# Expert weight loads: the first matrix's loads issued slot by slot from SyncE, the second matrix's from ScalarE's own queue

## What is computed

```python
def expert_block(args):
    xb, e = args
    gu = xb @ w_gu[e] + b_gu[e]                     # w_gu[e]: 1024 x 2048, float32
    g = jnp.minimum(gu[:, :D_EXPERT], SWIGLU_LIMIT)
    lin = jnp.clip(gu[:, D_EXPERT:], -SWIGLU_LIMIT, SWIGLU_LIMIT)
    act = g * jax.nn.sigmoid(SWIGLU_ALPHA * g) * (lin + 1.0)
    return act @ w_down[e] + b_down[e]              # w_down[e]: 1024 x 1024, float32
```

## Time and profile before

| | us |
|---|---|
| median of 3 runs | 1465.5 (1463.52 to 1466.69) |
| the profiled execution, its own time | 1465.08 |
| its span in the trace | 1463.2 |
| TensorE busy | 1431.0 (98% of the span) |
| VectorE, ScalarE, GpSimd busy | 499.0, 323.9, 276.9 |
| q1 (SyncE's loads) | 448.83 MB, 74.4% of 16 DMA engines' span |
| granted TensorE clock, mean | 0.997 |

### The profile page before, as it was taken

The page is one execution under the profiler, slowest core; times in us unless marked ns, Lnnn a source line. Parts: engine busy times, 40 slices in busy tenths (PEclk is TensorE's granted clock), DMA queues, the critical chain, the costliest instruction groups (busy, mean ns, idle before and its releaser), DMA issues.

```text
span 1463.2 us, 34048 instructions
## 1 busy us (share of the span) xinstructions
PE 1431.0 (98%) x14854; PEld 752.4 (51%) x14854; DVE 499.0 (34%) x715; ACT 323.9 (22%) x556; POOL 276.9 (19%) x360
## 2 busy tenths in 40 slices
PE   8999999999989999999999999999999999999997
PEld 7876588888863444444444444444444443333334
DVE  4848833324572223222222222232222222222233
ACT  6458842223121111111111111111111111111111
POOL 0000000000012222233222233222332222332211
PEclk9999999999999999999999999999999999999999
DMA  7330003323969599999999999999999999999987
GB/s 260 146 94 1 23 12 123 96 73 134 362 237 418 215 415 418 414 417 412 413 420 414 416 416 411 417 414 418 418 412 414 417 418 418 418 414 413 416 338 254
DMA packets 77595, 466.72 MB, mean 319 GB/s; under 512 B 23160, under 2 KB 31764, under 8 KB 52944
## 3 DMA queue, kind: packets, MB, share of 16 engines
q1 hardware_dynamic: 50528, 448.83, 74.4%
q0 software_dynamic: 18464, 16.94, 5.3%
q10 hardware_dynamic: 8560, 0.34, 0.3%
HBM read 456.69 MB, written 19.27 MB: 325 GB/s over the span
## 4 chain that ended last, share of the span: by engine, by line
PE 81%; DMA 14%; DVE 3%; issue 1%; ACT 1%; SPq 0%; POOL 0%; ACTq 0%; DVEq 0%; POOLq 0%
PE ps L1783 35%; PE ps L1799 19%; DMA dn_pair<-in_w_down 11%; PE ps L1433 7%; PE ps L1435 7%; PE ps L1434 7%; PE ps L1460 2%; DMA gu_pair<-in_w_gate_up 2%; PE ps L1586 1%; DVE head_max L1092 1%; PE ps L1542 1%; DVE probs L1110 1%; DMA xf<-x_rows 1%; DMA x_rows<-y_sb,sum_row 0%; PE ps L1689 0%
## 5 line engine op out<-in xcount | busy, mean ns | idle before, releaser
L1783 PE MATMUL ps<-gu_pair,xt 128*32 128x512 f32 x6144 | 668.4, 594 | 4.1 <-ACT ps L861 3.0
L1783 PEld LDWEIGHTS ps<-gu_pair,xt 128*32 128x32 f32 x6144 | 204.2, 110 | 448.0 <-issue 427.6
L1799 PE MATMUL ps<-dn_pair,act_t 128*32 128x256 f32 x6144 | 339.2, 379 | 2.5 <-DMA dn_pair<-in_w_down 2.0
L1799 PEld LDWEIGHTS ps<-dn_pair,act_t 128*32 128x32 f32 x6144 | 203.3, 110 | 146.6 <-issue 13.5
L1332 DVE TENSOR_SCALAR lin_sb<-ps 128x768 f32<-128x768 f32 x32 | 30.6, 958 | 584.7 <-ACT sg_sb L852 584.7
L852 ACT ACTIVATE sg_sb<-ps,limits 128x768 f32<-128x768 f32 x32 | 28.8, 901 | 593.5 <-PE ps L1783 593.5
L954 POOL DMA_INDIRECT x_rows<-y_sb,sum_row x93 | 147.0, 1581 | 37.7 <-issue 37.7
L931 POOL TENSOR_TENSOR mark_sb<-ones 1x1 f32<-1x1 f32 x93 | 30.0, 323 | 613.8 <-DVE y_sb L1348 608.7
L1433 PE MATMUL ps<-w_high,h_hi 128*128 128x512 f32 x352 | 138.2, 392 | 0.6 <-DVE mem_lo L1038 0.5
L1435 PE MATMUL ps<-w_high,h_lo 128*128 128x512 f32 x352 | 137.2, 390 | 0.0
L1434 PE MATMUL ps<-w_low,h_hi 128*128 128x512 f32 x352 | 137.0, 389 | 0.0
(11 more groups left out here) (249 smaller groups left out, 1002.6 us busy)
## 6 DMA issues: line engine op xcount, KB each, us to landing
gu_pair<-in_w_gate_up SPq DMA_DIRECT2D x128, 2048.0 KB, 29.0
dn_pair<-in_w_down SPq DMA_DIRECT2D x64, 2048.0 KB, 19.9
w_raw<-in_w_in SPq DMA_DIRECT2D x8, 2048.0 KB, 7.9
w_raw<-in_w_out SPq DMA_DIRECT2D x2, 2048.0 KB, 8.0
w_raw<-in_w_in SPq DMA_DIRECT2D x2, 1024.0 KB, 8.1
x_sb<-in_x SPq DMA_DIRECT2D x8, 256.0 KB, 7.8
w_raw<-in_w_mem_kv SPq DMA_DIRECT2D x1, 2048.0 KB, 12.6
x<-in_x SPq DMA_DIRECT2D x4, 512.0 KB, 5.3
```

What stands on the lines that cost most here:

```text
L1783: last = nc.tensor.matmul(ps[quarter(q), g, :], xt[:, g, k, :], w.rearrange("p (h n) -> p h n", h=2)[:, :, q * QCOLS:(q + 1) * QCOLS], sta ...
L1799: last = nc.tensor.matmul(ps[quarter(q), bank + g, 0:QCOLS], act_part(2 * c + h, g), dn_w[c][:, h * D + q * QCOLS:h * D + (q + 1) * QCOLS] ...
```

## The change

The second-matrix loads are taken out of SyncE's program and put into ScalarE's: `next_dn` in the loop, after `seed(j + 2)`, with the same waits for `down(j)`'s parts, and once more after the loop for job 31. They go through ScalarE's own hardware queue (q10). SyncE keeps the first-matrix loads; their waits from the second turn on are 4 parts lower, and the first turn of the loop is written out ahead of it.

```diff
--- before.py
+++ after.py
@@ -628,23 +628,25 @@
             sp.wait_ge(gate_t_ps, 1)
             load_gu(e_one, 1, GU_PAIRS - 1)
             pairs_but_one = sp.value_load(job_table[0:1, 1, 1:2], min_val=MIN_PAIRS - 1, max_val=NJ // 2 - 1)
-            with sp.Fori(0, pairs_but_one) as i:
+
+            def next_gu(i, b, e_gu):
+                for m in range(GU_PAIRS):
+                    wait_part(sp, i, b * PARTS - DN_PARTS + 2 * m + 1)
+                    load_gu(e_gu, b, m)
+
+            e_two = sp.value_load(job_table[0:1, 0, 2:3], min_val=0, max_val=N_EXP - 1)
+            for m in range(GU_PAIRS):
+                wait_part(sp, 0, 2 * m + 1)
+                load_gu(e_two, 0, m)
+            e_three = sp.value_load(job_table[0:1, 0, 3:4], min_val=0, max_val=N_EXP - 1)
+            next_gu(0, 1, e_three)
+            with sp.Fori(1, pairs_but_one) as i:
                 for b in range(2):
                     e_gu = sp.value_load(job_table[0:1, 0, bass.ds(i * 2 + b + 2, 1)], min_val=0, max_val=N_EXP - 1)
-                    e_dn = sp.value_load(job_table[0:1, 0, bass.ds(i * 2 + b + 1, 1)], min_val=0, max_val=N_EXP - 1)
-                    for m in range(GU_PAIRS):
-                        wait_part(sp, i, b * PARTS + 2 * m + 1)
-                        load_gu(e_gu, b, m)
-                    for m in range(DN_PAIRS):
-                        wait_part(sp, i, stream(b, KD + 2 * m + 1))
-                        load_dn(e_dn, m)
-            e_last = sp.value_load(job_table[0:1, 0, bass.ds(pairs_but_one * 2 + 1, 1)], min_val=0, max_val=N_EXP - 1)
+                    next_gu(i, b, e_gu)
             wait_part(sp, pairs_but_one, stream(0, KD - 1))
             for t in range(TB):
                 sp.dma_start(down_bias[N_EXP * t:N_EXP * (t + 1), :], b_down[0]).then_inc(down_bias_in, 16)
-            for m in range(DN_PAIRS):
-                wait_part(sp, pairs_but_one, stream(0, KD + 2 * m + 1))
-                load_dn(e_last, m)
             sp.wait_ge(act_ready, pairs_but_one * 2 + 2)
             sp.dma_start(final_gain[:], norm_final.rearrange("(a n) -> a n", a=1).to_broadcast([P, D])).then_inc(fgain_in, 16)
             sp.wait_ge(added, pairs_but_one * (32 * TRIOS) + (16 + 16 * TRIOS))
@@ -860,6 +862,9 @@
                     act.wait_ge(gs_ready, j)
                 nc.scalar.activation(ps[:, 0:TRIOS, :], bias_sb[:].rearrange("p (a h) n -> p a (h n)", a=1).to_broadcast([P, TRIOS, COLS]),
                                      ACT.Copy).then_inc(seeded, 1)
+
+            def next_dn(e, m):
+                act.dma_start(dn_pair[m][:], wdn[e, m, :, :]).then_inc(dn_in[m], 16)
 
             def keep_gate(j, b):
                 nc.scalar.activation(y_gate[:, b:b + 1, :], slot_gates[:, bass.ds(j, 1), :], ACT.Copy).then_inc(gate_kept, 1)
@@ -892,10 +897,18 @@
                     wait_part(act, i, stream(b, KD - 1))
                     sigmoid(j + 1)
                     seed(j + 2)
+                    e_dn = act.value_load(job_table[0:1, 0, bass.ds(j + 1, 1)], min_val=0, max_val=N_EXP - 1)
+                    for m in range(DN_PAIRS):
+                        wait_part(act, i, stream(b, KD + 2 * m + 1))
+                        next_dn(e_dn, m)
             keep_gate(pairs_but_one * 2, 0)
             act.wait_ge(act_ready, pairs_but_one * 2 + 1)
             wait_part(act, pairs_but_one, stream(0, KD - 1))
             sigmoid(pairs_but_one * 2 + 1)
+            e_last = act.value_load(job_table[0:1, 0, bass.ds(pairs_but_one * 2 + 1, 1)], min_val=0, max_val=N_EXP - 1)
+            for m in range(DN_PAIRS):
+                wait_part(act, pairs_but_one, stream(0, KD + 2 * m + 1))
+                next_dn(e_last, m)
             act.wait_ge(y_ready, pairs_but_one * 2 + 1)
             keep_gate(pairs_but_one * 2 + 1, 1)
             nc.scalar.activation(mark_act[:], ones[0:1, 0:1], ACT.Sqrt).then_inc(last_gate_kept, 1)
```

## The result

The changed kernel takes 1469.82 us, median of 7 runs (1469.29 to 1471.6), against 1465.5 (7 runs, 1463.52 to 1466.9): a ratio of 1.0031, 95% interval [1.0021, 1.0041]. It is slower by 0.3%, where 1459.0 and a gain of 0.4% were forecast. Its profiled execution took 1469.55 us, with a span of 1467.7.

A forecast was written before the change was run, and what follows sets the result against it. TensorE bounds the kernel until transfers win in the last quarter. Loop -6.95 with up to 0.5 given back, ScalarE, adds and tail 0: -6.5 taken, from 1465.5 to 1459.0 us, range 1456.5 to 1467.

The forecast's parts named there:

- What bounds the kernel: Loop: TensorE at 30.96 us a job, then transfers in the last quarter; 6.95 us lost to loads.
- The earlier waits: Near 480 us: the DMA gap gets filled once, so all later loads land 16.6 to 17.9 us sooner.
- a rival's mechanism: Uneven queue sharing: second-matrix pairs wait behind first-matrix ones, late 17 jobs later instead of 21; 1465 to 1468, chance 0.06.
- The second queue, its loads: Loop: second-matrix pairs land in time; last first-matrix pair just in time, costing nothing to 0.5 us; no bandwidth gained.
- The rival with the largest chance: Loop transfers lose some rate, or part of the gap stays; 1% less rate gives 1468.4; chance 0.24.
- ScalarE's new work: Two load issues per job fall in ScalarE's idle time after seed; taken as nothing.
- The adds: GpSimd's adds in the loop land in 21 us against 25.2 allowed; hidden, taken as 0.
- The price of that rival: Adds set the loop's pace: y_sb slips every job, 35 us at the 26.4 bound, 1494; chance 0.08.
- The tail: After down(30): 30.8 us, unchanged; earlier final gain worth nothing to 0.4 us, taken as nothing.
- The chance of 0.16 for slower: Whole kernel slower: 0.08 from lost transfer rate plus 0.08 from the adds setting the pace.

The follow-up runs named there:

- the two kernels in mixed order: Kernel before plus early waits, one queue, two of four first-matrix pairs behind second-matrix ones from job 12; final gain late or early: 1461.07, 1460.57 us.
- after_gathers_later: Changed kernel with GpSimd's gathers held back until VectorE has done turn_quarters, 6 us into a down: 1476.72 us, 1.0076 of the kernel before.
- before_gathers_at_clamp: Kernel before with the gathers held back until 2.6 us before the end of gate_up: 1465.84 us, 1.0000 of the kernel before.
- early_one_queue_gathers_later: Kernel before with the earlier waits, all loads in one queue, and the gathers held back behind turn_quarters: 1468.86 us in one run.

## Why the prediction was wrong

- **What bounds the kernel**: right. 6.95 us of waits for loads in the loop, and 928.8 us is what it takes without; the two kernels in mixed order reached it, and the one without the adds.
- **The earlier waits**: right. The share near 480 went from 0.17 to 1.00, and later loads came sooner. That this half alone would bring nothing, as the second matrix gets stuck behind the first, was in the text as a rival's mechanism, with job 19; it measured as job 19, and 1.0009.
- **The second queue, its loads**: right as to the loads. No second-matrix pair was late in the loop, and the last first-matrix pair wasn't either. The rival with the largest chance, a lost rate of the DMA engines, did not come. I had forecast that it would be just in time; it came well ahead, since nothing moves from 1415 to 1425. Of the Trainium skill (DMA: Bandwidth & Descriptors, Issuing engines are not separate DMA queues) the runs agree that the second queue brings no bandwidth: 416 GB/s against 418, and 1.0034 by itself.
- **ScalarE's new work**: right, no wait for it was seen.
- **The adds**: this is the step that failed; the term stands as 0 in the sum. I wrote "Hidden, with 4 to spare", from 21 us of landing against 25.2. It was 26.3. The figure it came from was misread: 15.9 is the median of the last two adds, and `take_y` waits for the last, which took 17.4 (17.2 to 18.7 over the loop of the kernel before, but for 19.6 in the first job). By the same working the estimate is 17.4 + 6 = 23.4, still hidden but with 1.8 to spare, and the bound is 17.4 + (17.4 - 5.4) = 29.4. That the bound in the text, 26.4, lies so near to the measured 26.3 is luck. I took the value below the bound because the second queue is full only half of the time from issue to landing. That was worked out for an early job, with adds issued at once after `y_sb`. The adds did hold in the early jobs and fell behind from 810 on, when the first-matrix queue had piled up. What I left out is that the transfers of both queues stretch as the backlog grows, and that the gathers stand in the same queue as the adds. That these two make up the difference is argued, not measured.
- **The price of that rival**: wrong in mechanism. I had `y_sb` slip in every job and TensorE with it, 35 us. In fact TensorE doesn't need `y_sb` for another 18 us, the slipping stops at about 15 (14.44 at 1099, 15.57 at 1131), and the price is paid by something that I hadn't on the list: gathers pushed into a `down`, 0.5 us each. It stops because the two paces have met: from 1004.99 to 1384.61 `y_sb` comes every 31.6 us, and from 1015.73 to 1393.73 TensorE's turn, with the pauses, takes 31.5. Where the slack was used up, in after_gathers_later, TensorE did wait as the rival says, at 33.25 us a turn.
- **The tail**: booked at nothing. A pair for job 31 is issued only 5.2 us before the end of `down(30)`, too late once `down(30)` no longer waits itself, and it met the final gain, which SyncE, no longer held by loads, issued 0.7 us ahead of it. `down(31)` then began late and ran in part at the lower clock. The tail is 0.8 and 2.8 us longer in the two traces; it isn't more, as before it waited for the last adds and for the rows read back.

The sum in traces, from `gate_up(2)` to the end: loop 936.4 (935.75 before; 928.8 forecast at best), tail 31.6 (30.8 before). That makes 1.4 us in the first trace and 4.3 in the second, 0.65 and 1.45 of them in the loop; the measured difference of the medians is 4.3. Against the forecast (929.25 and 30.8) the loop is 7.1 and 7.9 us longer: that is the pauses, and they are the larger part of what the forecast missed. How many `down`s a gather hits varies, and what makes one execution lose more than another was not settled.

The chance of 0.16 for slower was too low: even with the misread 15.9 the bound (26.4) was above what the ring allows (25.2), and I gave it 0.08.

## What to carry to other kernels

Before a stream of loads gets a queue of its own, look who else is in the DMA engines: small transfers that land in 17.4 us beside one full queue may need 26 beside two, and a ring through them (issue, landing, next issue) has to have room for that under full backlog, not as it stands in an early job. Take the landing of the transfer that the wait is for, not the median of a group. Where one queue is late only for one kind of load, reordering within that queue (here: two of four first-matrix pairs behind the second-matrix ones, with the earlier waits, which alone gave nothing) gave 0.36%, with the adds in time. When an engine off the path slips, follow what it issues to where it lands in time: its work may hit the bound engine there though nothing waits for it.

## What the runs showed of the hardware

- Issuing an indirect gather from GpSimd (1.00 to 1.03 us on the engine) can stop TensorE for about 0.5 us with no wait between them: 0.52 us a job over 30 `down`s. It happened where the third gather of a group, now and then the second, ended 1.6 to 4.6 us into a `down`; not at 0.4 us into a `down` (before_gathers_at_clamp), not at 1.35 (1079.39 + 1.01 in the changed kernel), and not in the middle of a `gate_up`, where the kernel before has them. About 1 us into a `gate_up` the weight loads stood idle for up to 0.6 us, but turns still took 30.96 us (560.06 to 714.86 in early_one_queue_gathers_later). The adds, issued 2 to 8 us into a `gate_up` in the kernel before, caused none. What the two share wasn't found.
- The landing of a job's last add went from 17.4 us beside one full load queue to 26.3 beside two, and it is 5.4 in the tail.
- The start of the loop moves by up to 3.8 us (495.97 to 499.78) between executions with nothing of it in the program. The late starts go with a granted TensorE clock of 0.68 between 418 and 434, most of the early ones with 1.00; TensorE had been busy for all of 410 to 420 in the changed kernel's trace (0.68), and for 9.38 us of it in that of the kernel before (1.00).
